# Five projection tiles, the sample's chunk first, and stage borders rearranged, in one layer of a gated linear-attention trunk

## The reference

```python
h = rmsnorm(x, norm_pre)
proj = h @ w_in                  # q, k, v, z of GLA; pool u, z; q, k, v, a, b, z of gated DeltaNet; 3 x 1024 gates
y_gla  = (head_rmsnorm(gla_recurrence(q, k, v, logf, s_gla)) * silu(gla_z)) @ gla_wo
y_pool = (pool_mix(pool_u) * silu(pool_z)) @ pool_wo
y_gdn  = (head_rmsnorm(gdn_recurrence(...short_conv(qkv)..., s_gdn)) * silu(gdn_z)) @ gdn_wo
m = sum(sigmoid(gate_b) * y_b for b in branches)
x = x + rmsnorm(m @ w_out, norm_post)
```

## Time and profile before

| | |
|---|---|
| median of three runs | 2521.21 us |
| the profiled execution | 2525.03 us, its span 2523.1 us |
| TensorE busy | 2446.3 us, 97% of the span |
| VectorE, ACT, POOL busy | 44%, 27%, 33% |
| mean granted TensorE clock | 0.983 |
| DMA over the span | 265 MB, 105 GB/s |

### The profile page before, as it was taken

One profiled execution on the slowest core, in us unless ns is written; L12 is line 12 of the kernel. 1 busy time (PEld: TensorE's weight loads), 2 busy tenths in 40 slices (PEclk: granted clock), 3 DMA queues, 4 the chain that ended last, 5 costly groups with the idle time before them and its releaser, 6 DMA issues. The chain is left out here.

```text
span 2523.1 us, 40394 instructions
## 1 busy us (share of the span) xinstructions
PE 2446.3 (97%) x15943; PEld 2314.1 (92%) x15943; DVE 1101.1 (44%) x1862; ACT 692.9 (27%) x1429; POOL 820.5 (33%) x711
## 2 busy tenths in 40 slices
PE   7999999999999999998999999999999979999998
PEld 7989999999999999997999998899999879999886
DVE  6620111224466563005666665566666444224332
ACT  6211111111155531112322333223332243213221
POOL 1212211211121121124654565545655213334222
PEclk9989999999999999999999999999999879999999
DMA  5213512101111221331243225442233355543443
GB/s 165 74 69 111 214 52 76 43 34 60 43 52 52 77 77 70 114 100 54 83 114 113 81 81 188 144 114 81 81 92 104 126 179 181 202 170 128 155 150 96
DMA packets 200145, 264.99 MB, mean 105 GB/s; under 512 B 16176, under 2 KB 175296, under 8 KB 194432
## 3 DMA queue, kind: packets, MB, share of 16 engines
q1 hardware_dynamic: 200064, 263.86, 32.4%
HBM read 164.54 MB, written 99.29 MB: 105 GB/s over the span
## 5 line engine op out<-in xcount | busy, mean ns | idle before, releaser
L178 POOL TENSOR_TENSOR w_hi<-w_raw,zero 128x1024 fp32r<-128x1024 f32 x77 | 148.3, 1927 | 1169.9 <-PE dense L348 826.6
L346 PE MATMUL dense<-h_hi_first,w_hi 128*128 128x352 f32 x1032 | 342.2, 332 | 0.6 <-POOL w_lo L180 0.6
L347 PE MATMUL dense<-h_lo_first,w_hi 128*128 128x352 f32 x1032 | 335.1, 325 | 0.0
L348 PE MATMUL dense<-h_hi_first,w_lo 128*128 128x352 f32 x1032 | 335.0, 325 | 0.0
L347 PE MATMUL dense<-h_lo_second,w_hi 128*128 128x352 f32 x1032 | 334.0, 324 | 0.0
L348 PE MATMUL dense<-h_hi_second,w_lo 128*128 128x352 f32 x1032 | 333.2, 323 | 0.0
L346 PE MATMUL dense<-h_hi_second,w_hi 128*128 128x352 f32 x1032 | 332.3, 322 | 0.0
L1368 PE MATMUL gate_bank<-h_hi_first,w_hi 128*128 128x352 f32 x768 | 276.5, 360 | 5.9 <-SPq L1283 5.1
L1368 PE MATMUL gate_bank<-h_hi_first,w_lo 128*128 128x352 f32 x768 | 249.6, 325 | 0.0
L1368 PE MATMUL gate_bank<-h_lo_first,w_hi 128*128 128x352 f32 x768 | 249.4, 325 | 0.0
L346 PEld LDWEIGHTS dense<-h_hi_first,w_hi 128*128 128x128 f32 x1032 | 195.8, 190 | 6.0 <-POOL w_lo L180 1.9
(11 more groups left out here) (237 smaller groups left out, 4658.9 us busy)
## 6 DMA issues: line engine op xcount, KB each, us to landing
w_raw<-in_w_in SPq DMA_DIRECT2D x77, 512.0 KB, 6.1
rows_then_inputs<-scratch_feat SPq DMA_DIRECT2D x16, 1856.0 KB, 9.1
scratch_feat<-row_y SPq DMA_DIRECT2D x28, 1056.0 KB, 4.9
gate<-scratch_gates SPq DMA_DIRECT2D x12, 2112.0 KB, 8.7
scratch_gates<-gate_row SPq DMA_DIRECT2D x96, 176.0 KB, 1.9
o_raw<-scratch_branch_out SPq DMA_DIRECT2D x6, 2112.0 KB, 12.9
scratch_merged<-merged SPq DMA_DIRECT2D x48, 176.0 KB, 1.8
rows_then_inputs<-in_x_prompt SPq DMA_DIRECT2D x16, 512.0 KB, 3.5
```

The lines of the kernel that those rows point to most:

```text
L178: nc.gpsimd.tensor_tensor(self.hi[:, p], raw, zeros, ALU.add).then_inc(self.high_ready, 1)
L346: nc.tensor.matmul(out, w_hi[:, p, k], h_hi[:, k, cols], start=(k == 0), stop=False)
L347: nc.tensor.matmul(out, w_hi[:, p, k], h_lo[:, k, cols], start=False, stop=False)
L348: mm = nc.tensor.matmul(out, w_lo[:, p, k], h_hi[:, k, cols], start=False, stop=(k == KD - 1))
```

## The change

- The project stage has five token tiles instead of six: 416, 416, 448, 416, 416 tokens. The middle one lies half in each half of h, and its moving operand is one access pattern over two pieces of 224 columns. Banks alternate over blocks too. The opening's schedule follows: tile 0 needs four norm tiles instead of three.
- The last two early gate blocks are made for the second half of the tokens alone there, six tiles of 352. Their first half goes to the chunk stage.
- The chunk stage takes the sample's chunk first, with 48 k-steps of gate products like the others, and then the 16 prompt chunks. Every chunk has gate products, the last one has all of them between its levels (8, 7, 7 k-steps at levels 4, 5, 6) and none in its closing part. The states are stored after the sample's chunk, and VectorE waits for these stores in the next chunk before it sets the states to zero. The swap is in the ninth chunk, and SP marks its first piece good before it waits for the last gate row.
- The rows of the sample's chunk and of the first prompt chunk are loaded in the project stage, as two chunks' rows were.
- SP doesn't wait for the last gate rows' stores at the end of the project stage; the engines wait for them in the chunk stage (rows_stored). At the end of the chunk stage SP doesn't wait for outputs and states; it does so in the closing stage before the second fetch of branch outputs, and VectorE at m = 4.
- In the last chunk SP fetches wo block 0, the branch outputs and wo block 1; ACT makes three high parts and VectorE three low parts there (EarlySplit). The gate halves are fetched first thing in the closing stage, ahead of wo blocks 2 and 3.
- The sample's token tile at the end is normed, added and stored in two halves by VectorE, not by VectorE and POOL. In the opening the gain is fetched ahead of the constants. Tensors of the closing stage move in memory, and rows of w_out are split one output block later.

```diff
+PROJ_TILES = 5
+MIDDLE = PROJ_TILES // 2
...
+PROJ_W = 416
+MIDDLE_PART = HALF_TOKENS - MIDDLE * PROJ_W
+SIG_W = 2 * MIDDLE_PART
+def width(t):
+    return 2 * MIDDLE_PART if t == MIDDLE else PROJ_W
+def span(t, shift=0):
+    start = t * PROJ_W + (2 * MIDDLE_PART - PROJ_W if t > MIDDLE else 0) + shift
+    return slice(start, start + width(t))
...
+    def tile(self, k, t):
+        if t == MIDDLE:
+            at = self.starts[0] + k * HALF_TOKENS + MIDDLE * PROJ_W
+            step = self.starts[1] - self.starts[0] - MIDDLE * PROJ_W
+            return bass.AP(self.words[:, :].tensor, at, [[self.row, P], [step, 2], [1, MIDDLE_PART]])
+        half, start = (0, t * PROJ_W) if t < MIDDLE else (1, MIDDLE_PART + (t - MIDDLE - 1) * PROJ_W)
+        return self.halves[half][:, k, start:start + PROJ_W]
...
-    todo = [(t, f, k) for t in range(TILES) for f in range(2) for k in range(KD)]
+    todo = [(t, f, k) for t in range(PROJ_TILES) for f in range(2) for k in range(KD)]
...
-    while todo and len(now) < STEPS and j >= -(-(todo[0][0] + 1) * TW // P) - 1 + 2:
+    while todo and len(now) < STEPS and j >= -(-span(todo[0][0]).stop // P) - 1 + 2:
...
+    out = dense[:, (t + p) % 2, 0:width(t)]
     for k in range(KD):
-        cols = slice(t % 3 * TW, (t % 3 + 1) * TW)
-        out = dense[:, t % 2, 0:TW]
-        nc.tensor.matmul(out, w_hi[:, p, k], h_hi[:, k, cols], start=(k == 0), stop=False)
-        nc.tensor.matmul(out, w_hi[:, p, k], h_lo[:, k, cols], start=False, stop=False)
-        mm = nc.tensor.matmul(out, w_lo[:, p, k], h_hi[:, k, cols], start=False,
+        nc.tensor.matmul(out, w_hi[:, p, k], hi.tile(k, t), start=(k == 0), stop=False)
+        nc.tensor.matmul(out, w_hi[:, p, k], lo.tile(k, t), start=False, stop=False)
+        mm = nc.tensor.matmul(out, w_lo[:, p, k], hi.tile(k, t), start=False,
                               stop=(k == KD - 1))
...
-    with pe.Fori(0, 1 + EARLY_GATES // 2) as i:
...
+    with pe.Fori(0, EARLY_GATES // 2) as i:
...
+    for n in range(6):
+        u, t = n // 3, n % 3
+        if t == 0:
+            pe.wait_ge(w_split, F_LATE - 1 + u)
+        pe.wait_ge(act_free, (A_GATE + EARLY_GATES - 2) * PROJ_TILES + n - 1)
+        out = dense[:, (n + 1) % 2, 0:TW]
+        for k in range(KD):
+            cols = slice(t * TW, (t + 1) * TW)
+            nc.tensor.matmul(out, w_hi[:, 1 - u, k], hi[1][:, k, cols], start=(k == 0), stop=False)
+            nc.tensor.matmul(out, w_hi[:, 1 - u, k], lo[1][:, k, cols], start=False, stop=False)
+            mm = nc.tensor.matmul(out, w_lo[:, 1 - u, k], hi[1][:, k, cols], start=False, stop=(k == KD - 1))
+        mm.then_inc(dense_ready, 1)
...
-    for c in range(2):
-        first.load(sp, d, c, c)
-    for n in range(EARLY_GATES - 4, EARLY_GATES - 1):
+    first.load(sp, d, CHUNKS, 0, NS_)
...
-    sp.wait_ge(gate_stored[1], EARLY_GATES // 2 * 16)
-    sp.wait_ge(gate_stored[0], (EARLY_GATES // 2 + TILES // 2 - 1) * 16)
...
+    def rows_stored(self, eng):
+        for p, count in enumerate(self.STORES):
+            eng.wait_ge(self.gate_stored[p], count * 16)
...
+    if swap and T == TILES - 1:
+        good(0)
...
+    first.rows_stored(sp)
+    sp.wait_ge(state_zero, 2)
...
+    gate_traffic(0, 0, None)
+    store_states(0, "new_gdn_sample", "new_gla_sample")
+    store(0, CHUNKS, NS_)
+    load(1, 0)
...
+    gate_traffic(CHUNKS // 2, 0, 1, swap=True)
+    for t in range(1, 3):
+        if t == 2:
+            outputs(CHUNKS // 2, CHUNKS // 2 - 1, 0)
+        good(t)
...
+    gate_traffic(CHUNKS - 1, 1, 1)
+    store(CHUNKS - 1, CHUNKS - 2)
+    gate_traffic(CHUNKS, 1, None)
+    sp.wait_ge(out_stored, 16 * 5)
+    sp.wait_ge(outg_stored, 16 * 5)
     for q in range(2):
...
     late.load_in_chunk_phase(sp, d)
...
-    sp.wait_ge(state_stored, 10 * 16)
-    sp.wait_ge(out_stored, 16 * (CHUNKS + 2))
-    sp.wait_ge(outg_stored, 16 * (CHUNKS + 2))
...
+    store_states(CHUNKS, "new_gdn_prompt", "new_gla_prompt")
+    store(CHUNKS, CHUNKS - 1)
...
+    chunk(SAMPLE, FIRST)
+    chunk(FIRST, SECOND)
+    with eng.Fori(1, CHUNKS // 2) as i:
         chunk((i * 2, i, 0, P), (i * 2 + 1, i, 1, P))
         chunk((i * 2 + 1, i, 1, P), (i * 2 + 2, i + 1, 0, P))
-    i = CHUNKS // 2 - 1
-    sample = (CHUNKS, i + 1, 0, NS_)
-    chunk((CHUNKS - 2, i, 0, P), (CHUNKS - 1, i, 1, P))
-    chunk((CHUNKS - 1, i, 1, P), sample)
...
-    gate_products(3)
+    gate_products({4: 8, 5: 7, 6: 7}.get(l, 3) if then is None else 3)
...
+    if then is None and l > 2:
+        gates_out(c, l - 1)
+    elif l in (4, 5):
+        gates_out(c, l - 2)
...
+    before(act, "outg_ready", c)
+    early_split.high(act, nc, late)
...
+    dve.wait_ge(state_stored, 5 * 16)
+    nc.vector.memset(state[:, :, :], 0.0)
+    nc.vector.memset(gla_state[:, :, :], 0.0).then_inc(state_zero, 1)
...
+    if then is None:
+        early_split.low(dve, nc, late)
...
-    for m in range(2):
-        self.load_wo(sp, d, m)
+    self.load_wo(sp, d, 0)
     self.load_o(sp, d, 0)
-    for half in range(2):
-        self.load_gates(sp, d, 0, half)
+    self.load_wo(sp, d, 1)
...
+    def high(self, act, nc, late):
+        act.wait_ge(late.o_landed, 16)
+        nc.scalar.copy(self.o_hi[0][:, :, :], late.o_raw[:, 0:4]).then_inc(self.o_high, 1)
+        act.wait_ge(late.wo_landed[0], 16)
+        nc.scalar.copy(self.wo_hi[:, :, :], late.wo_ring[:, 0]).then_inc(self.wo_high, 1)
+        nc.scalar.copy(self.o_hi[1][:, :, :], late.o_raw[:, 4:8]).then_inc(self.o_high, 1)
...
+    def low(self, dve, nc, late):
+        def difference(lo, raw, hi):
+            return nc.vector.tensor_tensor(lo[:, :, :], raw, hi[:, :, :].bitcast(F32), ALU.subtract)
+        dve.wait_ge(self.o_high, 1)
+        difference(self.o_lo[0], late.o_raw[:, 0:4], self.o_hi[0]).then_inc(self.o_split, 1)
+        dve.wait_ge(self.wo_high, 1)
+        difference(self.wo_lo, late.wo_ring[:, 0], self.wo_hi).then_inc(self.wo_split, 1)
+        dve.wait_ge(self.o_high, 2)
+        difference(self.o_lo[1], late.o_raw[:, 4:8], self.o_hi[1]).then_inc(self.o_split, 1)
...
+    sp.wait_ge(late.out_stored, 16 * (CHUNKS + 2))
+    sp.wait_ge(late.outg_stored, 16 * (CHUNKS + 2))
...
+    for half in range(2):
+        late.load_gates(sp, d, 0, half)
...
+    if m == KD - 4:
+        dve.wait_ge(late.out_stored, 16 * (CHUNKS + 2))
+        dve.wait_ge(late.outg_stored, 16 * (CHUNKS + 2))
+        dve.wait_ge(late.state_stored, 10 * 16)
...
+    if n < P:
+        dve.wait_ge(x_landed[p], (CHUNKS // 2 + 1) * 16)
+        dve.wait_ge(stored[p], CHUNKS // 2 * 16)
+        for half in range(2):
+            at = slice(half * 512, half * 512 + 512)
+            nc.vector.scalar_tensor_tensor(normed[0:n, p, at], tokens_bank(p)[0:n, at], better,
+                                           gain[0:n, at], ALU.mult, ALU.mult).then_inc(normed_ready, 1)
+            dve.wait_ge(normed_ready, t + 1 + half)
+            nc.vector.tensor_tensor(result[0:n, p, at], normed[0:n, p, at], x_in[0:n, p, at],
+                                    ALU.add).then_inc(last_ready, 1)
+        return
...
-    token_tile(CHUNKS, CHUNKS // 2, 0, NS_)
...
+    sp.dma_start(gain[:, :], d["norm_pre"].to_broadcast([P, DM])).then_inc(gain_landed, 16)
```

More of the change, by code:

```diff
@@ L24 @@
 LEVELS = 7
-ROW = 2144
+ROW = NT + 2 * 15
 POOL_HALO = 15
@@ L358, in forget_gates @@
                 def forget_gates(b):
-                    for t in range(TILES):
-                        n = b * TILES + t
+                    for t in range(PROJ_TILES):
+                        n = b * PROJ_TILES + t
                         at_least(pe, side_free, n - 1)
-                        nc.tensor.matmul(side[:, n % 2, 0:TW], wf2[:, b * P:(b + 1) * P],
-                                         X[0:16, 0, t * TW:(t + 1) * TW], start=True, stop=True) \
+                        nc.tensor.matmul(side[:, n % 2, 0:width(t)], wf2[:, b * P:(b + 1) * P],
+                                         X[0:16, 0, span(t)], start=True, stop=True) \
                             .then_inc(side_ready, 1)
@@ L422, in pool_map @@
                     pe.wait_ge(pool_d_ready, g + 1)
-                    for t in range(TILES):
-                        n = (2 + g) * TILES + t
+                    for t in range(PROJ_TILES):
+                        n = (2 + g) * PROJ_TILES + t
                         pe.wait_ge(side_free, n - 1)
-                        nc.tensor.matmul(side[:, n % 2, 0:TW], pool_w[:, g], X[:, 1, t * TW:(t + 1) * TW],
+                        nc.tensor.matmul(side[:, n % 2, 0:width(t)], pool_w[:, g], X[:, 1, span(t)],
                                          start=True, stop=True).then_inc(side_ready, 1)
@@ L443, in two @@
                             return
-                        for t in (2 * tile, 2 * tile + 1):
+                        for t in range(2 * tile, min(2 * tile + 2, PROJ_TILES)):
                             if isinstance(j, int) and j == 0 and t < 2:
```

(41 more changed lines are left out.)

535 lines of the change are left out of this document (280 added, 255 removed).

## The result

The median of six executions is 2506.1 us (2499.09 to 2527.18), against 2521.67 us for the kernel before (2517.78 to 2522.30, six executions): a ratio of 0.9946, 95% interval 0.9928 to 0.9964. It is faster, as forecast, but by 16 us instead of 33, and outside the range of 2477 to 2502. The spread is new: the kernel before stays within 4.5 us, the changed one spreads over 28, and the slowest of its executions is the profiled one, 2527.18 us. So the profile after shows what an unlucky execution loses, and why it does is the case's main lesson.

What follows compares the result with a forecast made beforehand. TensorE, 97% busy over 2523.1 us, was taken as the bound. Terms -13.8 - 23.0 + 1.5 - 2.3 - 2.2 + 8 - 1.3 = -33.1 us gave 2491.9 against the profiled 2525.0, median 2488, range 2477 to 2502.

Steps and rivals of the forecast that it cites:

- 13 steady chunks: Chunk stage: 13 chunks were to keep their old time of 51.47 us each, 669.1 us together.
- the rivals: Five alternative outcomes: no closing wait 0.15, costlier chunk order 0.2, no width gain 0.05, slow middle tile 0.04, change ineffective 0.06.
- the swap chunk: Chunk stage, chunk where h halves swap: 55.9 us (53 to 58.3) instead of 58.33, three pieces still moving at queue pace.
- The tile width: Project stage: five tiles save 24 fixed parts of 13.3 ns, 0.32 us a block, -13.8 us over 43 blocks.
- The rival for this: Project stage: 13.3 ns is no fixed part, a block keeps its 23.04 us, total 2502 us; chance 0.05.
- the moved gate products: Project stage: first halves of blocks 43 and 44, 144 matmuls, leave for the chunk stage, -23.0 us there.
- the border: Project to chunk stage: SP's wait for the last gate stores is dropped, gap about 3.6 us, -2.3 (0 to -3).
- the middle tile: Project stage's 448-column tile: reading its operand in two runs of 224 costs 0, at most 10 us over 1032 matmuls.
- the last chunk and border: End of chunk stage: 65 us (60 to 71), the end chain running without gate products beside it.
- the closing wait: Closing stage's start: TensorE waits 6.4 us because wo block 2 queues behind the gate halves, +8 (0 to +10).
- the last tile: Sample's token tile at the end: VectorE norms and adds in halves, -1.3 us (-0.5 to -2).
- the sample's chunk: Start of chunk stage: 49 us (45 to 53), 23.0 of it gate products and 20.7 its own.

Runs made afterwards that it cites:

- e1: Changed kernel with 128 semaphore increments put at the start of TensorE's project program, shifting its later code by 128 instructions: median 2510.49 us, ratio 0.9958.
- e10: Like e5 but with half the shift, 64 instructions in place of 128: median 2526.77 us, ratio 1.0019.
- e5: Changed kernel with the 128-instruction shift made of already-met waits in TensorE's opening gaps, in place of increments: median 2500.84 us, ratio 0.9918.
- e8: Changed kernel with matmul runs added behind its end, operands from two tensors and steps of 1024 or 1056: 512 columns take 226.7 or 232.2 ns.
- e9: Changed kernel with matmul runs added behind its end, varying operand start and step: without a step, 416 columns take 186.6 to 193.3 ns.
- e4: Changed kernel with runs of 96 matmuls of 352 to 512 columns added behind its end: 161.1 ns at 352, 232.2 at 512.
- e3: e1 with SP issuing the second gate half after wo blocks 2 and 3 at the closing stage's start: median 2506.27 us, ratio 0.9946.
- e6: e5 with SP marking the swap's third h piece good before issuing the next rows' loads: median 2496.53 us, ratio 0.9897.
- e2: Kernel before the change, with the same 128 increments at the start of TensorE's program: median 2550.78 us, ratio 1.0125.

## Why the prediction was wrong, point by point

**The sum.** Set against the profiled execution, 2491.9 was forecast and 2527.2 came, 35.3 more. It divides at the stages' first products: the first gate product was to come at 1151.35 - 37.6 = 1113.8 and came at 1115.91, +2.2; the chunk stage was to take 891.5 and took 2039.90 - 1115.91 = 924.0, +32.5; the rest was forecast to 0.6 us.

**The failed step** is the chunk stage's 13 steady chunks at 51.47: the prediction took the loop's time over unchanged, as its work was unchanged, and never asked whether the loop's code stays resident where it comes to lie. None of the rivals held this. It is 27 us of the 35 in the profiled execution (first to last output 865.45 there, 838.17 in e1): some 22 in the steady chunks and 6 in the swap chunk. It is 26 us in e10's median, but only 5 in the changed kernel's own (2506.1 against e5's 2500.8), as five of its six executions took 2499 to 2507 us and will have fetched in few turns or none, to judge by e8 and e9 (inferred: only one of the six was profiled).

**The other 13 us of the median's miss of 18** are there without the fetching. Against e5's profiled 2498.2 the forecast was 6.3 too low, of which 5.3 are the chunk stage (896.8 against 891.5, the swap and sample chunks below). The rest is the step from an execution to a median: the forecast took its profiled execution for 3.8 over the median, and e5's is 2.7 under. e5's median lies in the range that was given; the changed kernel's does not.

**The tile width** was the other mis-sized term: -13.8 forecast, 43 x 0.12 = -5.2 measured. The line went through two rows whose operands lie differently, 352 columns of h and 512 columns of w_out; with h's layout throughout (e4) the slope is 0.444 ns a column and little stays fixed. The two widths that were wanted lie above the line, by 2.0 and 3.6 ns. The rival for this had 0.05 and should have had much more. By the rule of the page cited in the prediction (the Trainium skill, TensorE: Matmul & The Clock Gate, "Wait — 56ns, not 53.3ns?") 0.06 us a block were to be saved, nearer to the measured 0.12 than the 0.32 of the line; its absolute times (149 and 216 ns) are met by no row here.

**What hid that error**: three things in the same stage that were not priced gained. TensorE's 4.2 us of standing at the sums of squares went. The first product came 1.1 us later instead of 1.5; VectorE's wait for the gain fell from 8.4 to 5.5. And some 2 us more went in places that were not traced. The stage as a whole was forecast to 2.4 us; it was right by accident, and only the time of one block showed it.

**Right in mechanism and size**: the moved gate products (last 23.0 us of the stage now where 46.2 stood); the border (3.7 us from start to start where it was 6.25, -2.5 against -2.3); the middle tile, near 0 (2.2 ns); the first prompt chunk, 52.04 against 52.5; the last chunk and border, 2039.90 less 1977.12 = 62.8 against 65; the closing wait, 6.94 against 6.4 with its order of the queue (e3 takes 4.7 of e1's 7.34 away), though its own terms give 19.9 - 13.4 = 6.5 and its 2.5 for a first latency names no row (a wo block took 4.4 to land, some 2.4 over its 2.0); the last tile, 9.5 us from the last matmul's start to the end where it was 11.1, -1.5 against -1.3.

**Wrong in size**: the sample's chunk took 51.7 instead of 49. The swap chunk was to fall to 55.9 and rose to 59.6 to 60.5 without the fetching (e8, e5, e1; 58.33 before): the mark of the first piece did come earlier (3.04 to 1.23 us of wait), but the third piece's mark stayed behind the loads' issue, and TensorE waited 4.4 to 5.5 there instead of 2.0. e6 shows that SP's order was the limit, not the pace of the queue, as the prediction had it.

## What to carry to other kernels

A loop of unchanged work isn't an unchanged loop when code is added or taken away anywhere ahead of it: look at the instruction queue's packets in the loop's window before you read its chunks' times, and if the body is fetched anew, move it (here by 128 instructions in an idle gap) before tuning anything else. One profiled execution without packets does not clear a place: the same code had 0, 17, 40 and 48 in four; a narrow spread of many executions is the better sign. A price per matmul holds for the operand layout of its row; take it from the same tensor, measure the widths between as well as the ends, or read a block's time between two evictions. Where an engine marks data for another, put the mark ahead of the issues that can stand behind a full queue.

## What the runs showed of the hardware that was not expected

- A loop of 1674 TensorE instructions is kept, or fetched in 9 packets of 16 KB a turn: 0 packets in 600 us in e1, e5 and the kernel before, 48 in the changed kernel's profiled execution and in e10. A turn that fetches has a wait of 2.9 to 4.2 us, followed by a stretch at half the clock, and its chunk takes 3 to 7 us longer. Its place in the code shifts the odds (e1, e5, e10), and at one place it can lose the loop (e2) or get it back (e9).
- A matmul of 512 columns at full clock takes 226.6 to 233.4 ns and one of 416 takes 186.6 to 193.3, as the moving operand's start varies. Starts that are best for one width are not for another (e9, one execution).
- 128 semaphore increments on TensorE take 20.5 us; 128 instructions with two waits each that are already met, in the gaps of the opening, took no time that can be seen (e5).
